# One token step on one core: 142 instead of 128 of the small group's value rows on VectorE, and half of the second dense tile's first one-hot blocks on GpSimd

## The reference

```python
xn = rmsnorm(x, g_mix);  xr, yr, ca, cb, ga, gb = split(xn @ w_in)
branch_a = (rglru(conv4(xr)) * gelu(yr)) @ w_a
branch_b = silu(layernorm(conv31(ca * sigmoid(cb)))) @ w_b
x = x + (sigmoid(ga) * branch_a + sigmoid(gb) * branch_b) @ w_out
q = rmsnorm(x, g_ffn) @ w_q                  # 8 heads, two halves of 128
v1, i1 = top_k(s1, 16);  v2, i2 = top_k(s2, 16)   # s = q halves @ keys
sv, si = top_k(v1[:, None] + v2[None, :], 16)
e = i1[si // 16] * 128 + i2[si % 16]         # 16 experts of 16384, each head
act = gelu(einsum('thkd,td->thk', u_tab[e], xn))
x = x + einsum('thk,thkd->td', softmax(sv) * act, v_tab[e])
y = rmsnorm(x, g_final)
```

## Time and profile before

| | us |
|---|---|
| median of 3 runs | 3907.44 |
| lowest, highest | 3903.29, 3908.87 |
| the profiled execution's own time | 3898.97 |
| span of its trace | 3897.2 |

### The profile page before, as it was taken

The page is one execution under the profiler, slowest core; times in us unless marked ns, Lnnn a source line. Parts: engine busy times, 40 slices in busy tenths (PEclk is TensorE's granted clock), DMA queues, the critical chain, the costliest instruction groups (busy, mean ns, idle before and its releaser), DMA issues.

```text
span 3897.2 us, 32153 instructions
## 1 busy us (share of the span) xinstructions
PE 2977.0 (76%) x10622; PEld 1821.6 (47%) x10622; DVE 2629.8 (67%) x3962; ACT 560.0 (14%) x1106; POOL 1433.1 (37%) x862
## 2 busy tenths in 40 slices
PE   6999988999978999996942222334169899999993
PEld 5989976555544555553521111212143334444441
DVE  3830034899877765465649899899976566665657
ACT  4520011222200000001010001223250000000000
POOL 0000002232344433243336666667522234433334
PEclk9999989999989999997976665666589999999997
DMA  7867757787699989897869999999758999999998
GB/s 197 238 187 240 242 178 272 240 300 267 244 362 383 384 331 383 283 350 290 329 266 392 390 391 385 361 379 366 290 195 354 361 408 420 421 421 421 421 421 353
DMA packets 461518, 1278.18 MB, mean 328 GB/s; under 512 B 24104, under 2 KB 335144, under 8 KB 335912
## 3 DMA queue, kind: packets, MB, share of 16 engines
q0 software_dynamic: 120528, 875.29, 56.0%
q1 hardware_dynamic: 327808, 390.63, 29.6%
q10 hardware_dynamic: 13064, 10.87, 0.8%
HBM read 1265.55 MB, written 12.00 MB: 328 GB/s over the span
## 4 chain that ended last, share of the span: by engine, by line
PE 39%; DMA 32%; DVE 17%; issue 7%; POOL 3%; ACT 1%; ACTq 0%; DVEq 0%; POOLq 0%; SPq 0%
PE ps L1615 25%; DMA region<-in_v_tab_dram,region 19%; PE ps L1599 11%; DVE region L1451 8%; DMA region<-in_u_tab_dram,region 4%; DMA region<-in_w_in_dram 4%; POOL region L635 3%; DVE region L1385 2%; DMA region<-in_w_q_dram 2%; DMA region<-scores_kept 1%; DVE region L1475 1%; DMA region<-in_w_b_dram 1%; PE ps L1810 1%; DVE region L1334 1%; DVE region L1331 1%
## 5 line engine op out<-in xcount | busy, mean ns | idle before, releaser
L635 POOL DMA_INDIRECT region<-in_u_tab_dram,region x544 | 897.7, 1650 | 1778.5 <-DVE region L1376 562.1
L1615 PE MATMUL ps<-region,region 128*128 128x160 f32 (+1 forms) x5120 | 1212.6, 399 | 85.5 <-DMA region<-in_w_in_dram 36.0
L1615 PEld LDWEIGHTS ps<-region,region 128*128 128x128 f32 x5120 | 847.9, 194 | 441.6 <-DMA region<-in_w_in_dram 46.9
L1451 DVE SCALAR_TENSOR_TENSOR region<-region,region 128x2048 f32<-128x2048 f32 x384 | 867.2, 2285 | 93.8 <-DMA region<-in_u_tab_dram,region 56.0
L1385 DVE SCALAR_TENSOR_TENSOR region<-region,region,region 128x2048 f32<-128x2048 f32 x256 | 601.6, 2350 | 480.5 <-DMA region<-in_v_tab_dram,region 474.1
L1840 PE MATMUL ps<-region,region 128*128 128x512 f32 x2048 | 896.7, 600 | 37.4 <-DMA region<-in_v_tab_dram 36.7
L635 POOL DMA_INDIRECT region<-in_v_tab_dram,region x288 | 527.4, 1831 | 666.7 <-DVE region L1385 610.5
L1840 PEld LDWEIGHTS ps<-region,region 128*128 128x128 f32 x2048 | 392.4, 192 | 541.1 <-issue 486.9
L1599 PE MATMUL ps<-region,region 128*128 128x160 f32 (+1 forms) x2048 | 477.5, 395 | 8.3 <-DVE region L1324 4.1
L1788 PE MATMUL ps<-region,region 128*128 128x512 f32 x256 | 181.2, 873 | 327.6 <-DMA region<-in_v_tab_dram,region 323.9
L1599 PEld LDWEIGHTS ps<-region,region 128*128 128x128 f32 x2048 | 336.1, 191 | 146.3 <-issue 8.2
(11 more groups left out here) (217 smaller groups left out, 1403.4 us busy)
## 6 DMA issues: line engine op xcount, KB each, us to landing
region<-in_w_in_dram SPq DMA_DIRECT2D x256, 512.0 KB, 4.7
region<-in_v_tab_dram SPq DMA_DIRECT2D x128, 1024.0 KB, 9.1
region<-in_w_out_dram SPq DMA_DIRECT2D x64, 512.0 KB, 4.6
region<-in_w_q_dram SPq DMA_DIRECT2D x64, 512.0 KB, 6.9
region<-in_w_a_dram SPq DMA_DIRECT2D x32, 512.0 KB, 4.9
region<-in_w_b_dram SPq DMA_DIRECT2D x32, 512.0 KB, 4.8
region<-in_u_tab_dram,region POOLq DMA_INDIRECT x544, 9.7
region<-in_x_prompt_dram SPq DMA_DIRECT2D x7, 1024.0 KB, 9.5
```

The costliest lines, as they stand in the source:

```text
L635: pool.indirect_dma_start(out=slot, out_offset=None, in_=rows_ap, in_offset=bass.IndirectOffsetOnAxis(ap=idx[:, k:k + 1], axis=0)).then_in ...
L1451: stt(out=u_b[s], in0=u_b[s], scalar=1.0, in1=xn_tile(UNITS_A + u), op0=ALU.mult, op1=ALU.mult, accum_out=dots[u % 2][:, k:k + 1]).then_in ...
L1615: last = mm(outs[n][:, 0:WIDTH[g]], wide[s][:, q, n * P:(n + 1) * P], rhs(k), start=(k == 0), stop=(k == n_k - 1))
```

## The change

- `ROWS_W` goes from 128 to 142, which is the number of steps from step 18 on. So each step from 18 to 159 has one value row. The 14 further rows (128 to 141) are of unit 8, the sample tile, and add to `xf[1]`.
- `ROWS_P` falls from 32 to 18: that many value rows are left to TensorE in the u stage. `ROW_AT` puts one at about every twelfth dot.
- `STEPS_2`, `STEPS_3`, `STEPS_4` are 48, 114, 134. The chunk stage has 34 steps (before 32), the branch stage 66 (72), the output stage 20 (22), the query stage 24 (18).
- For the odd batches of the second dense tile, `one_a` is made by GpSimd, with the same operation, four for a batch. Eight batches stand in GpSimd's program before the gather of row z = 7, four before z = 8, four before z = 9. TensorE waits for a semaphore of its own.

```diff
-ROWS_W = 8 * TOPK
+V_LAG = TOPK + 2
+ROWS_W = ROWS_A - V_LAG
...
+def on_pool(t, b):
+    return t == 1 and b % 2 == 1
...
+POOL_AT = [7 + max(0, b // 8 - 1) for b in range(BATCHES)]
...
-STEPS_1, STEPS_2, STEPS_3, STEPS_4 = 14, 46, 118, 140
+STEPS_1, STEPS_2, STEPS_3, STEPS_4 = 14, 48, 114, 134
...
+            def first_ones(b):
+                n = BATCHES + b
+                pool.wait_ge(turn_read, 2)
+                pool.wait_ge(built, n - 1)
+                for q in range(BATCH):
+                    col = BATCH * b + q
+                    last = nc.gpsimd.tensor_scalar(one_a[n % 2][:, q, :], count, turned[:, 0, col:col + 1],
+                                                   turned[:, 2, col:col + 1], ALU.is_equal, ALU.mult)
+                last.then_inc(pool_ones, 1)
+
             for z in range(P + V_LAG + 1):
+                for b in range(BATCHES):
+                    if on_pool(1, b) and POOL_AT[b] == z:
+                        first_ones(b)
...
-                        value_row(v, v, v, xf[0])
+                        value_row(v, v, v, xf[v // P])
...
+                if on_pool(t, b):
+                    return
...
-                pe.wait_ge(a_ones, n + 1)
+                if on_pool(t, b):
+                    pe.wait_ge(pool_ones, b // 2 + 1)
+                else:
+                    pe.wait_ge(a_ones, n + 1 if t == 0 else BATCHES + b // 2 + 1)
```

2 lines of the change are left out of this document (1 added, 1 removed).

## The result

The changed kernel takes 3965.38 us (median of 4 runs, 3954.97 to 3976.84) beside 3905.36 us for the kernel before on the same chip: a ratio of 1.0155, 95% interval 1.012 to 1.0189. That is 60 us slower, where 4 us slower was forecast, and outside the range of 3888 to 3928. The profiled execution took 3961.79 us, with a span of 3960.0.

What follows compares the result with a forecast made beforehand. TensorE's waits were taken to count before 1985 us, VectorE's or its gathers' to 2830, a batch's chain to 2898. Terms +7 + 6 + 5 - 12 - 2 = +4 on the median 3907.44 gave 3911 us, range 3888 to 3928.

Steps and rivals of the forecast that it cites:

- The second dense tile: Building that tile: GpSimd takes one-hot products from VectorE, 1.11 us a pair of batches, at most 2.9 us: -2 us.
- Rival C: Slower: GpSimd holds the second dense tile back; at 1.0 us an operation +19, in all +25, 3932; chance 0.08.
- The lock between VectorE and GpSimd: Building the second dense tile: three dots could each hold a batch back, turning the -2 into about +3.
- The query stage: 24 steps with 24 value rows; more transfers make TensorE's weights late: +5 us, bounds 0 and +10.
- The branch stage: Seven later pairs after the first merge: 8 or 9 value rows as before, TensorE didn't wait for VectorE: 0.
- The u stage: 14 gathers leave it, a third of VectorE's waits for u rows goes: -12 us, bounds -4 and -28.
- A: Faster: gathers set the u stage's pace, so 28 us go there; in all -21, 3886; chance 0.28 including values towards the forecast.
- D: Slower: the 14 rows only change place, u waits come from gather latency; -4 instead of -12, +12, 3919; chance 0.12.
- Layer norm and first merge: Chunk stage to first merge: VectorE starts the norm 15 us later, TensorE goes on 10 us late: +7 us, bounds +3 and +14.
- Output stage: Unit 9's routing moves behind block 13's addition, lengthening VectorE's way to the norm: +6 us, bounds +2 and +8.
- rival B: Slower: late norm, moved routing and full DMA in the query stage at their bounds, 30 us; in all +16, 3923; chance 0.14.

Runs made afterwards that it cites:

- The second buffer: Against the kernel with only GpSimd's 64 products added, GpSimd got two buffers in turn: build 105.6 to 73.0 us, whole 1.001 of the kernel before.
- rows alone: Kernel before with 142 of the small group's value rows on VectorE, old steps, no GpSimd products: 1.0036 (1.0022 to 1.0049).
- 114 rows: Kernel before with 114 instead of 128 of the small group's value rows on VectorE, 46 left to the u stage (output wrong): 0.9988 (0.9968 to 1.0008).
- rows and steps: Changed kernel without GpSimd's products, VectorE making all one-hot blocks; 142 value rows and new steps stay: 1.0066 (1.0042 to 1.009) against the kernel before.

## Why the prediction was wrong, point by point

**The second dense tile: the step that failed, +38.5 for -2.** Three things stood in it. (1) The operation: I took 0.35 us, "nearest the row of the same shape", a GpSimd operation that makes a mask and reads no per-partition scalars. The real one takes 0.82 us undisturbed and 1.1 in the mean, above even my upper bound of 0.7. (2) The window: I allowed GpSimd 3.83 - 1 = 2.8 us a batch. It is smaller, because GpSimd may only start when TensorE has finished the odd batch before: 2.0 to 2.4 us pass between its groups at the low clock and 1.45 at the high one, which leaves 1.5 to 2.4. The wait on `built` stood in the diff, and so did the one buffer; I priced the product in it at the high clock, as if the delay left the clock alone. (3) The clock: with a wait in each pair the granted clock of the stretch was 0.67 instead of 0.89, TensorE's product took 3.4 to 3.8 us in most pairs instead of 2.02, and it stands in the same chain. Rival C named the place and the sign, but even with 1.0 us an operation it gave +19, since it only counted the excess over a window that was itself too long. The second buffer shows that an operation as slow (0.97 us) costs 5 us when it needn't wait; 33 of the 38 us needed the one buffer: the series, the low clock, and row products that GpSimd had no lead to absorb.

The lock between VectorE and GpSimd stood beside the sum, not in it: three row products, each holding a batch back, that would turn the -2 into +3, so 5 us. Three groups did meet one, and between the batches they cost 6 us (105.6 to 99.3). The four behind the last batch were not thought of: GpSimd's last group took 11.14 us beside them, against 3.29 alone. The Trainium skill, "SBUF — State Buffer", section "Who interferes with whom", says that a VectorE instruction with two SBUF inputs and a GpSimd instruction that reads SBUF exclude each other. The trace agrees, with these two numbers and with the groups of 5.77 us beside one row product.

**The query stage, +13.6 for +5,** was a term of the right mechanism and the wrong size. Late weights cost 12.0 us instead of 5.6 (+6.4, near my 5), and TensorE's products took 5.7 us more in the stage (behind a wait of 5 us the next 16 matmuls took 3.0 us longer), which I had not counted. VectorE was early at the end, by 13.35 us of idle time where "under 10" was forecast.

**The branch stage, +8.8 for 0.** "TensorE didn't wait for VectorE: 0" was true of the later pairs and beside the point: it waited for weights, 33 us, with the DMA engines full, and 37.8 us in the changed kernel:

```profile
1150.00:1600.00 450.00, 416.81 (x1253) 239.98 (x1252) 312.16 (x358) 30.06 (x52) 182.06 (x113) 0.98 0.97 368
```

That is the kernel before, DMA share 0.97. I put a stage with late weights at nothing because its count of value rows stayed. The count did stay (58 value gathers after 56), and the stretch grew all the same: rows alone put it 13 us up, 114 rows 23 us down. That the rows do it is shown; by which way is not.

**The u stage, -10.3 for -12,** was right, and so was its working: the u waits fell by 14 us, a little over a third (the forecast had 24 us of them left, 22.1 were), and "rows alone" shows the same (22.5 us). Rivals A and D fall. (A's sum had set 10 us against the gain for the places that the forecast itself has at 18.)

**Layer norm and first merge, +7.5 for +7.** VectorE starts the norm 17.9 us later, of which 3.5 stood already at the group's first gate product (15 forecast), TensorE waits 4.2 us in the chunk stage (4.3). At the norm it waits 10.4 us instead of 5.0, where 10 us more had been forecast. The first merge scatters over 1128 to 1142 in kernels whose work up to there is the same, so that the agreement to half a microsecond is chance; the three kernels with 48 steps lie at 1139 to 1143, and the mechanism shows best in their norm.

**Output stage, +4.8 for +6.** Unit 9's routing does stand between the additions of blocks 13 and 14 (1769.2 to 1779.2), and TensorE's wait for the norm is 43.7 us instead of 33.2, where I had said 39.

Without the build the terms sum to +24, where +6 was forecast; "rows and steps" measures +26 by its ratio. So even without GpSimd's part the forecast of no change would have missed: by rival B's way, whose three places gave 26 us of its 30, and by the branch stage, which no rival had.

## What to carry to other kernels

When work is given to another engine, draw the cycle of buffer, producer and consumer before pricing the operation: with one buffer the producer's time and the consumer's add up. Here a second buffer gave back 33 us, and halving the producer's work 23. Look first whether the engine that is relieved sets the pace of the stage; here it didn't, and nothing could be won. And when rows are moved, look at both ends: a stage in which no engine waits for the moved work can still become longer through its waits for weights, as it did here, even with no more gathers issued in it.

## What the runs showed of the hardware

The same operation, a comparison and a product over 128x128 floats with two per-partition scalars, takes VectorE 1.11 us for four (0.28 each) and GpSimd 3.29 us for four (0.82): nearly three times as long. Beside four of VectorE's products over 2048 elements, GpSimd's four took 11.14 us. Beside one such product they took 5.77. And behind a wait of 5.07 us, with the granted clock at 0.50, 16 matmuls of TensorE took 8.39 us instead of 5.43, so that this late transfer cost more than half of its length once again.
